# The second tile's eight routing heads placed at every eighth value row of the first tile instead of every tenth

## What is computed

```python
q = (hf @ w_q).reshape(N, PEER_HEADS, 2, PEER_HALF)
s1 = jnp.einsum('nhd,hkd->nhk', q[:, :, 0], sub_k1)      # 128 scores per half
s2 = jnp.einsum('nhd,hkd->nhk', q[:, :, 1], sub_k2)
v1, i1 = lax.top_k(s1, 16); v2, i2 = lax.top_k(s2, 16)
cand = (v1[..., :, None] + v2[..., None, :]).reshape(N, 8, 256)
sv, si = lax.top_k(cand, 16)
idx = e1 * 128 + e2                                       # the experts chosen
gate = jax.nn.softmax(sv, axis=-1)
a = einsum('nhkd,nd->nhk', u_tab[idx], h)
coef = gate * gelu(a)
out = einsum('nhk,nhkd->nd', coef, v_tab[idx])            # 8 heads x 16 = 128 experts a token
```

## Time and profile before

| | |
|---|---|
| median of the runs | 4559.45 us |
| the profiled execution | 4551.36 us, of which the span is 4549.6 us |
| TensorE busy | 4042.5 us, 89% |
| VectorE busy | 3103.4 us, 68% |
| moved by DMA | 1529.03 MB, mean 336 GB/s |
| the chain that ended last | PE 55%, DMA 26%, DVE 7% |

### The profile page before, as it was taken

One profiled execution on the slowest core, in us unless ns is written; L12 is line 12 of the kernel. 1 busy time (PEld: TensorE's weight loads), 2 busy tenths in 40 slices (PEclk: granted clock), 3 DMA queues, 4 the chain that ended last, 5 costly groups with the idle time before them and its releaser, 6 DMA issues.

```text
span 4549.6 us, 60824 instructions
## 1 busy us (share of the span) xinstructions
PE 4042.5 (89%) x23368; PEld 3497.3 (77%) x23368; DVE 3103.4 (68%) x4561; ACT 924.5 (20%) x1339; POOL 1321.7 (29%) x822
## 2 busy tenths in 40 slices
PE   7999999999899989999798999999999997676565
PEld 7999999999789987887687878887787775343222
DVE  7434344444647577888687885888898656798776
ACT  4334434323433421011001000000000004000100
POOL 0000000000000013434442432444454431567664
PEclk9999999999899999999899999999999998787777
DMA  6555677775365569999999999999999996999998
GB/s 220 198 207 191 213 287 288 282 262 182 110 243 210 202 240 422 416 400 409 415 407 373 403 423 417 407 423 423 423 413 423 424 403 281 413 391 400 422 422 353
DMA packets 303267, 1529.03 MB, mean 336 GB/s; under 512 B 36394, under 2 KB 108538, under 8 KB 134948
## 3 DMA queue, kind: packets, MB, share of 16 engines
q0 software_dynamic: 114288, 830.54, 44.1%
q1 hardware_dynamic: 188772, 695.78, 40.2%
HBM read 1450.06 MB, written 76.13 MB: 335 GB/s over the span
## 4 chain that ended last, share of the span: by engine, by line
PE 55%; DMA 26%; DVE 7%; issue 4%; DVEq 2%; POOL 2%; ACT 2%; ACTq 0%; SPq 0%; POOLq 0%
PE psum L588 29%; PE psum L3345 10%; PE psum L654 9%; DMA sb_raw_u<-in_wstream 9%; DMA sb_ring<-in_peer_v,sb_idx_all 9%; DMA sb_raw<-in_wstream 5%; POOL sb_ring L3155 2%; DMA sb_ring<-in_peer_u,sb_idx_all 2%; PE psum L3606 2%; PE psum L2342 2%; DVE sb_acc_b L3502 1%; DVE sb_ring L3176 1%; DVEq L2371 1%; DVE sb_split L572 1%; ACT sb_split L568 1%
## 5 line engine op out<-in xcount | busy, mean ns | idle before, releaser
L588 PE MATMUL psum<-sb_actr,sb_split 128*128 128x264 f32 x7344 | 911.8, 286 | 26.1 <-DVE sb_split L572 15.1
L588 PEld LDWEIGHTS psum<-sb_actr,sb_split 128*128 128x128 f32 x7344 | 901.6, 190 | 30.9 <-issue 20.5
L572 DVE TENSOR_TENSOR sb_split<-sb_raw,sb_split 128x2048 fp32r<-128x2048 f32 x201 | 460.6, 2291 | 625.9 <-ACT sb_split L568 625.3
L3061 POOL DMA_INDIRECT sb_ring<-in_peer_u,sb_idx_all x256 | 428.4, 1674 | 1081.3 <-PE psum L588 512.9
L3181 DVE SCALAR_TENSOR_TENSOR sb_acc<-sb_ring,sb_coef,sb_acc 128x2048 f32<-128x2048 f32 x256 | 601.7, 2351 | 161.0 <-DMA sb_ring<-in_peer_v,sb_idx_all 146.4
L3176 DVE CUSTOM_DVE_ANT_0 sb_ring<-sb_ring,sb_htok 128x2048 f32<-128x2048 f32 x264 | 595.5, 2289 | 159.3 <-DMA sb_ring<-in_peer_u,sb_idx_all 129.9
L3061 POOL DMA_INDIRECT sb_ring<-in_peer_v,sb_idx_all x256 | 422.7, 1651 | 635.0 <-DVE sb_acc L3181 553.5
L3606 PE MATMUL psum<-sb_ring,sb_diag 128*128 128x512 f32 x512 | 356.4, 860 | 241.4 <-DMA sb_ring<-in_peer_v,sb_idx_all 234.2
L3502 DVE SCALAR_TENSOR_TENSOR sb_acc_b<-sb_ring,sb_coef_b,sb_acc_b 128x2048 f32<-128x2048 f32 x192 | 451.2, 2350 | 126.0 <-DMA sb_ring<-in_peer_v,sb_idx_all 112.8
L3155 POOL DMA_INDIRECT sb_ring<-in_peer_v,sb_idx_all x256 | 438.6, 1713 | 250.9 <-DVE sb_acc_b L3502 127.9
L3345 PE MATMUL psum<-sb_h2b,sb_raw 128*128 128x256 f32 x2048 | 458.1, 383 | 24.7 <-DMA sb_raw<-in_wstream 24.7
(11 more groups left out here) (455 smaller groups left out, 4337.1 us busy)
## 6 DMA issues: line engine op xcount, KB each, us to landing
sb_raw<-in_wstream SPq DMA_DIRECT2D x398, 1024.0 KB
sb_raw_u<-in_wstream SPq DMA_DIRECT2D x64, 1024.0 KB
sb_states<-in_state SPq DMA_DIRECT2D x32, 512.0 KB, 3.9
sb_states_t<-in_stateT SPq DMA_DIRECT2D x32, 512.0 KB, 4.4
out_gla_s<-sb_states SPq DMA_DIRECT2D x32, 512.0 KB, 3.0
dram_z<-sb_zst SPq DMA_DIRECT2D x121, 132.0 KB
dram_z_b<-sb_zst SPq DMA_DIRECT2D x65, 128.0 KB
sb_vrow<-dram_v SPq DMA_DIRECT2D x8, 1024.0 KB, 5.5
```

What stands on the lines that cost most here:

```text
L572: nc.vector.tensor_tensor(split[:, slot, 1, :], raw[:, slot, :], split[:, slot, 0, :], ALU.subtract).then_inc(lo_ready, 1)
L588: last = nc.tensor.matmul(psum[:, bank, 0:ntok], w[a], acts(b, kt), start=(i == 0 and a == 0 and b == 0), stop=(i == len(kts) - 1 and a == 1))
L3061: nc.gpsimd.indirect_dma_start(ring[g % RING][:], None, ins[table], bass.IndirectOffsetOnAxis(ap=col, axis=0)) \
```

## The change

`head_beside` is called with t = 1 for the heads of tile 1 and t = 2 for those of the samples. The spacing was 10 rows for the first and 8 for the second, and is 8 for both:

```diff
             def head_beside(t, n):
 
-                k, rest = divmod(n - 12, (10, 8)[t - 1])
+                k, rest = divmod(n - 12, 8)
                 if rest == 0 and 0 <= k < PH:
                     if k == 0:
                         dve.wait_ge(sc_loaded, 16 * t)
                     top_head(dve, t, k)
```

## The result

Over 19 runs each, the kernel after takes 4567.03 us in the median (4558.79 to 4570.64) and the kernel before, on the same chips, 4559.35 us. The ratio is 1.0013, with a 95% interval of 1.0007 to 1.0019: the change costs 3 to 9 us, about 6. The working is another matter: the sum was +1.2 us, by a gain of 6.95 us that is given back, and neither half of that is in the trace.

A forecast was written before the change was run, and what follows sets the result against it. The prediction took full DMA engines to bound the kernel from the late merges on; 0.4 (early heads) + 0.8 (transfers, with 6.95 us gained and given back) = +1.2 us, rounded to 4560 us, range 4550 to 4568.

The forecast's parts named there:

- a gain of 6.95 us: Late merges: without the head of k = 42, a 4.66 us bank wait and 2.29 us of slow products go.
- part one: Outputs k = 0 to 15: a sixth head costs nothing directly, +0.4 us net through idle DMA.
- Part two: Outputs k = 16 to 47: heads at k = 19 and 28 replace 22, 32 and 42; merges end 6.95 us earlier.
- rival three: Rows without heads, k = 28 to 44: slower GpSimd gathers shrink 6.95 us to some 3; still 4560 us; chance 0.10.
- the full clock: Last TensorE pair of the merges: takes 7.17 us instead of 9.46 at a lower granted clock, saving 2.29 us.
- Part three: Transfers around and behind the merges: -2.2 + 2.7 + 0.3 = +0.8 us, and the 6.95 us are given back.
- The hole at the head of k = 28: Idle DMA during that head in the merges: 5 us instead of 2.3 before, so +2.7 us.
- The giving back: Sum behind the output blocks: full DMA engines cancel the 6.95 us; TensorE waits about 13 us instead of 6.
- Full transfers: From the late merges to 3786 us the DMA engines are full, so earlier merges bring only recovered idle, 2.2 us at most.
- Rival two: Six-slot ring stalls: new gaps at k = 5 and 28 paid in full, +8.7 us, 4568 us; chance 0.14.
- the hole at the head of k = 5: Idle DMA during that early head: 3.6 to 6 us in the forecast, 6 us in full by Rival two.
- Rival one: The merges' gain survives: -6.95 us, 4552.5 us, or -14.7 and 4545 us with the early wait and clock; chance 0.20.

The follow-up runs named there:

- e1: Half of the change: first six heads where the change puts them, last two left at k = 32 and 42; ratio 0.9995 to the kernel before.
- e7: Kernel after with the gates of outputs 32 to 47 loaded at least eight outputs before use, all bytes kept; 4559.95 us, ratio 1.0001 to the kernel before.
- e3: Kernel after without the gate loads of k = 32 to 47, so part of the merge is wrong; ratio 0.9990 to the kernel before.
- e9: Kernel before with the gates of outputs 32 to 47 loaded ahead of time, nothing else changed; ratio 1.0001 to the kernel before.
- e10: e1 with the gates of outputs 32 to 47 loaded ahead of time; ratio 1.0003 to the kernel before.

## Why the prediction was right, and where it was wrong

**The edit and part one** hold. The sixth head in k = 0 to 15 was to cost 0.4 us. TensorE's wait for weights in stage one went from 5.32 to 6.03 us, and the block behind it starts 0.7 us later, counted from the first score product (2405.86 - 2240.82 = 165.0 against 2402.80 - 2238.46 = 164.3). e1 carries it to the end: no loss that can be measured.

**Part two, as far as the head of k = 28**, holds as well: a bank wait of 2.6 us was forecast and 2.72 measured. Ahead of the last pair none was left, as forecast.

**The step that failed** is the next one: "From the k = 32 of before on VectorE is at the same place as before", and from it "The merges end at about 2570 instead of 2577 us". They end at 2586.66, or 7.4 us later than before instead of 6.95 earlier, counted as above. From k = 32 on TensorE waits 14.3 us instead of 8.4: 6.0 us of waits for a bank became 2.7, as the forecast had it, and 1.3 of waits for weights, which it had shrinking to 0.1, became 9.3. I followed VectorE's work and TensorE's banks, and treated the gates as if they were always there, because nothing in the trace of before waits for one. Yet I had the number that speaks against it. With VectorE taking a row every 3.12 us, 1 MiB each, and a weight block of 1 MiB and two gates of 128 KB every 6.9 us, the asking rate is 336 + 152 + 38 = 526 GB/s against 423 that flow when the engines are full. Before, a head of 9.35 us came every ten such rows and let the engines catch up; after, there is none for the seventeen rows of k = 28 to 44. I noticed that VectorE takes rows without a pause, and priced it as GpSimd's problem (rival three) and not as that of the queue in front of the gates and weights. e7 measures what the step left out, with every byte in place: 9.6 us of the stretch. Even then the gain was smaller than forecast: e7's merges take 2.2 us less than the kernel before's, not 6.95. The bank wait of 2.69 us was in the forecast; the 3.04 for weights was not, and of the 2.29 us that the full clock was to give back, 1.0 came (57.5 us of products against 58.5 before).

**Part three.** The hole at the head of k = 28 was forecast at 5 us instead of 2.3. In the stretches after:

```profile
2510.00:2515.00 5.00, 2.78 (x13) 2.10 (x12) 4.45 (x9) 0.00 (x0) 0.00 (x0) 1.00 0.61 252
2515.00:2520.00 5.00, 4.50 (x13) 3.73 (x14) 4.80 (x7) 0.00 (x0) 1.87 (x2) 0.66 0.61 185
...
2590.00:2595.00 5.00, 5.00 (x24) 4.37 (x23) 2.01 (x1) 0.00 (x0) 2.98 (x2) 0.95 0.51 172
2595.00:2600.00 5.00, 5.00 (x25) 4.41 (x24) 4.17 (x5) 0.00 (x0) 0.00 (x0) 1.00 0.97 385
2600.00:2605.00 5.00, 5.00 (x25) 4.41 (x24) 4.09 (x5) 0.00 (x0) 3.39 (x2) 1.00 0.76 264
```

The first two give 2.0 + 2.8 = 4.8 us. The 2.2 us of idle between 2565 and 2590 us, which I had as regained, fell only to 1.0 (407 GB/s), and the other three rows give 3.0 + 0.5 + 1.9 = 5.3 us of new idle behind the merges. While VectorE waited for gates it took no rows, the ring was full, and when the waits ended nothing was under way. That is the second half of the failed step: the late gates first find the DMA engines too full and then leave them empty. Summed over 2240 to 2610 us in rows of 5 us the engines idle 35 us after and 27 before, of which those 5.3 lie behind the merges' end. The 8 us are close to the 7.7 by which the sum comes later: on a path that is full of transfers afterwards they stay in the time.

**The giving back.** TensorE's wait at the sum was to grow from 5.97 to 13 us. It fell to 4.48, since the merges came later and not earlier. Whether a gain in the merges would be given back shows in the three runs whose merges end over 2 us earlier than before. At the merges' end, at the sum and at the table's first block e3 is 4.7, 2.5 and 2.6 us ahead of the kernel before, e1 2.3, 2.0 and 0.2, e7 2.2, 1.2 and -0.5; e3 waits 8.22 us at the sum. So a tenth to a half is given back by the sum, and in e1 and e7 the rest by the table; these are differences of single profiles, and I had expected all of it at the sum. "Full transfers" was too strong a reading, but the direction holds: in the time e3's gain over before is 0.0 to 0.2%.

**The rivals.** Rival two had the direction and nearly the size (+8.7 us) by a mechanism that isn't there: the hole at the head of k = 5 is 1.5 us and not 6 (10 us at 359 GB/s from 2315 us on), and stage one lost 0.7. Rival one fell in the kernel after; e7 shows it only within the uncertainty of the times. Rival three's long gathers did come, five of them from 2531.78 us on, but VectorE waited for gates and not for rows. I also read the gathers too simply: that of 2525.62 us starts 0.04 us after a row pass does and takes 0.94 us all the same, so a pass alone doesn't make a gather long, and "the gather would wait to the pass's end" isn't what this row shows. The time of 4560 us is right to 7 us by luck, because the error of 14 us in the merges (+7.4 instead of -6.95) was half covered by the 6.95 that I had given back. By the time both +1.2 and 6 us are "no change"; by the mechanism they are opposite.

No version here beats the kernel before by more than its measurement can tell. e1 and e3 come nearest, and e3 leaves work out.

**Open.** Whether the loads are late for want of lead or for the queue time that the gates take up isn't told apart, as said at e7. Why the clock stays low longer behind the sum, which costs the 2 us between there and the table (138.4 before, 140.4 after), isn't shown. The kernel after and e7 weren't run side by side on one chip, so that the gates' worth in the time rests on each one's ratio to the kernel before, and their intervals overlap; the gain of 9.6 us stands on the stretches of one profile each, with e9 and e10 as the pairs in which nothing was to be gained and nothing was.

## What to carry to other kernels

A small load that no engine waits for is not free of price: write down its lead (here four outputs, 13.8 us) next to its time from issue to landing, and ask what that time becomes if the change takes away a pause. Work of an engine that seems to be in the way can be what lets the transfers catch up; taking it out, or moving it earlier, can turn its time into waits unless the loads are asked for earlier too. And ask of a shared queue what each load takes up in it, from landing to landing: here the small ones took over half as much as the large one.

## What the runs showed of the hardware

A load of 128 KB took 6.5 us from issue to landing with the DMA engines busy but with pauses, and 14 to 15 us in the median, up to 20.5 (the gate issued at 2540.38 us), behind a queue of 1 MiB rows and weight blocks. I had expected a load an eighth of the size to be fast whatever stood beside it; the weight blocks of 1 MiB took 16.3 us in the same stretch, hardly more. A load waits here for what stands ahead of it and not for its own bytes. And it holds up what stands behind it by more than its bytes: from landing to landing 2.8 us for 128 KB, 4.9 to 5.0 for 1 MiB, beside a steady stream of row gathers.

The Trainium skill, DMA: Bandwidth & Descriptors, section Latency and other measured facts, gives the access latency of HBM as 0.2 us on average and 2 us at high load. The landings of the gates are seven times the larger figure, so by that figure alone a lead of four outputs is ample; the rows decide, and what they show is the queue and not the memory's latency.
